# A hybrid decoder step: prompt attention heads whose transposes and products use four other PSUM banks, with ScalarE's exponentials moved ahead of its evictions

## The chip, the cores and the metric

The kernel runs on one core of one Trainium2 chip. The metric is the device time of one execution in microseconds (us). Five engines work side by side, each through its own list of instructions: TensorE (PE, with weight loads shown apart as PEld), VectorE (DVE), ScalarE (ACT), GpSimd (POOL) and SyncE (SP, which here only issues DMAs). They meet only at semaphores.

## The reference

One layer of a decoder trunk is applied to a prompt of 512 tokens and to a sample group of 8 sequences with 8 new tokens each, with the same weights. The part that matters here is the attention of the prompt. Every query keeps its 128 best keys (chosen by the indexer), and the softmax runs over these:

```python
logits = jnp.einsum('bthd,btkhd->bthk', q, k_sel).astype(jnp.float32) * ATT_SCALE
bias = rel_bias[rel_bucket(q_pos[None, :, None] - idx)]
logits = logits + jnp.swapaxes(bias, -1, -2).astype(jnp.float32)
logits = jnp.where(valid[:, :, None, :], logits, -jnp.inf)
p = jax.nn.softmax(logits, axis=-1).astype(v_sel.dtype)
out = jnp.einsum('bthk,btkhd->bthd', p, v_sel)
```

There are 8 heads of 128 columns, all in float32. Around it stand one wide input projection, the same attention of the sample group over 2,048 cached positions (paged keys and values, 64 MB each), a spatial gating branch, output projections and a convolutional feed-forward network.

## The kernel before

The program is written out engine by engine, in one block for each; nothing is scheduled automatically. The stages in the order of TensorE are: input transposes, indexer, the q, k and v projections, the eight prompt heads, the sample attention (two groups G, each with a loop over 17 pages of keys and four loops over pages of values), and the rest.

PSUM has eight banks of 128 x 512 float32. Banks 0 to 3 form two pairs; column tiles and row tiles of the projections fill them in turn (`pbank`, `ptile`). Banks 4 to 7 are single banks (`bank`), which are handed out strictly in the order of a list made at the top of the function: `single.add` gives each fill the next of the four banks. A fill waits until the previous use of its bank is drained (`claim`), and signals `single_filled` when done. The names of fills in this stage are `pl` (logits of head h, row block r), `pt` (the probabilities transposed) and `pv` (the product with the values).

The eight heads ("heads stage") are pipelined over h = 0 to 8. A head has four blocks of 128 query rows; block r sees 128 x (r + 1) keys (the causal half). For each h:

- TensorE (loop at L1214): logits of head h+1 (four matmuls, L1204), the product of head h-1 with the values (four matmuls, L1222), then ten 128 x 128 transposes of head h's probabilities (L1230).
- VectorE (L1861): reciprocal of the sums (L1862), four normalisations of the probabilities (L1865), then `prompt_max` for head h+1: for each row block, logits plus a bias mask with a running maximum (L1852), and one negation of the four maxima (L1856), which signals `max_ready`.
- ScalarE (L1560): eviction of the head's output (L1565, "oa"), four evictions of the transposed probabilities into the buffer `PT` (L1572), then the four exponentials of head h+1 (L1541), which signal `exp_done`.
- GpSimd (L899): the bias masks `MB` for the next head, four row blocks in six instructions (L905 to L909), each when VectorE has read the same block of the head before.

The logits buffers `L`, the maxima `MX`, `NM`, the sums `SU` and reciprocals `RC` exist twice (h % 2); `PT` and `MB` exist once. Behind the last head, TensorE does 32 steps of a "side" projection (`side_parts('start')`, columns `ga`), GpSimd clears `QB` (L933), ScalarE fills it (L1582), and the key loop begins with VectorE's transposes of key pages (L1910).

Apart from the heads, `sample_mask` (L1824 to L1843, 15 VectorE instructions, of 128 x 1032 in the larger ones) turns the sample group's best lists into a mask. It stands on VectorE between `prompt_max(0)` and the first normalisation.

## Time and profile before

| what | value |
|---|---|
| time of three runs | 1479.3, 1481.48 and 1484.05 us, median 1481.48 us |
| the profiled execution's own time | 1478.58 us |
| its span, first to last instruction | 1476.9 us |
| TensorE busy | 93% of the span |
| VectorE, ScalarE, GpSimd busy | 53%, 28%, 23% |
| heads stage | about 320 to 393 us of the span |
| mean granted TensorE clock | 0.969 |

The profile is of one execution. Busy shares are means over stages with different limits. The granted clock is a share of 2.4 GHz: 1.00 is 2.4 GHz and 0.50 is 1.2 GHz. "Idle before" is the time the engine stood idle directly before an instruction, with the instruction that released it. In the trace, a float32 matmul is two records, so a group of four matmuls is shown as x8.

### The profile page before, as it was taken

Reading aid. Unit: us, or ns where it says so; the run is one execution under the profiler, and the core shown is the slowest. Engines: PE = TensorE matmul, PEld = TensorE weight load, DVE = VectorE, ACT = ScalarE, POOL = GpSimd, SP = SyncE. Lnnn points to the kernel's source line nnn. Section 1 sums busy time; section 2 is a strip of 40 time slices with the busy share of each in tenths; the row PEclk is TensorE's granted clock in tenths of the full one; section 3 lists DMA queues with packets and bytes.
Section 4 is the critical chain, followed back from the end, with each engine's and each line's share of the span. In section 5 each row is a group of like instructions: output and inputs, shape, how many; then the busy total and the mean of one; then the engine's idle time right before and its main releaser. Section 6 shows DMA issues by size and latency. Waiting matters only on the chain.

```text
span 1476.9 us, 33784 instructions
## 1 busy us (share of the span) xinstructions
PE 1369.3 (93%) x14554; PEld 1228.4 (83%) x14554; DVE 788.7 (53%) x1117; ACT 417.2 (28%) x596; POOL 337.0 (23%) x427
## 2 busy tenths in 40 slices
PE   6989998987888999889999999999999999999997
PEld 4966798974677876578876698999999999999997
DVE  5278779444188820088820037444666676762221
ACT  4243322234521131011131141223333333332221
POOL 3613323424332100032100001322222222210000
PEclk8899999999999999999999999999999999999998
DMA  6415223230399899999899884142432223332332
GB/s 182 138 48 163 60 68 133 68 122 1 127 346 374 312 354 403 402 364 343 315 332 391 349 303 159 48 142 86 150 84 76 76 81 86 86 123 82 84 86 81
DMA packets 170624, 266.81 MB, mean 181 GB/s; under 512 B 19866, under 2 KB 136011, under 8 KB 161259
## 3 DMA queue, kind: packets, MB, share of 16 engines
q1 hardware_dynamic: 149275, 174.13, 35.1%
q0 software_dynamic: 14320, 78.22, 13.9%
q10 hardware_dynamic: 6880, 12.29, 2.4%
q8 instruction: 115, 1.88, 0.5%
q14 instruction: 34, 0.28, 0.1%
HBM read 240.30 MB, written 24.18 MB: 179 GB/s over the span
## 4 chain that ended last, share of the span: by engine, by line
PE 76%; DVE 10%; ACT 4%; DMA 4%; issue 3%; POOL 1%; SPq 1%; ACTq 0%; DVEq 0%; POOLq 0%
PE PS L1024 15%; PE PS L1026 14%; PE PS L1025 14%; PE PS L1257 5%; PE PS L1289 4%; PE PS L1366 3%; PE PS L1368 3%; PE PS L1367 3%; PE PS L1068 3%; DMA R<-in_cache_v 3%; DVE SR L1820 3%; DVE STG L1819 3%; PE PS L1069 2%; PE PS L1070 2%; PE PS L1222 1%
## 5 line engine op out<-in xcount | busy, mean ns | idle before, releaser
L1024 PE MATMUL PS<-xn_hi,WH 128*128 128x288 f32 (+1 forms) x1424 | 431.9, 303 | 6.2 <-DVE xn_lo L1702 3.8
L1026 PE MATMUL PS<-xn_hi,WL 128*128 128x288 f32 (+1 forms) x1424 | 421.7, 296 | 1.2 <-issue 1.2
L1025 PE MATMUL PS<-xn_lo,WH 128*128 128x288 f32 (+1 forms) x1424 | 421.7, 296 | 0.4 <-issue 0.3
L1024 PEld LDWEIGHTS PS<-xn_hi,WH 128*128 128x128 f32 (+1 forms) x1424 | 268.2, 188 | 24.4 <-issue 11.6
L1025 PEld LDWEIGHTS PS<-xn_lo,WH 128*128 128x128 f32 (+1 forms) x1424 | 268.6, 189 | 1.3 <-issue 1.3
L1026 PEld LDWEIGHTS PS<-xn_hi,WL 128*128 128x128 f32 (+1 forms) x1424 | 268.5, 189 | 1.4 <-issue 1.4
L604 DVE TENSOR_TENSOR WL<-W,WH 128x2048 fp32r<-128x2048 f32 (+2 forms) x73 | 154.8, 2120 | 181.2 <-ACT WH L1420 181.1
L1420 ACT ACTIVATE WH<-W 128x2048 fp32r<-128x2048 f32 (+2 forms) x81 | 144.9, 1789 | 105.1 <-PE PS L1368 74.8
L1460 ACT ACTIVATE STG<-PS 128x576 f32<-128x576 f32 (+2 forms) x44 | 23.4, 531 | 342.7 <-PE PS L1026 194.3
L657 POOL DMA_INDIRECT R<-in_cache_k,KROW x64 | 64.4, 1006 | 235.8 <-PE PS L1289 99.6
L1910 DVE STREAM_TRANSPOSE R<-R 128x2048 f32<-128x2048 f32 x42 | 96.0, 2295 | 20.1 <-PE PS L1257 16.2
L1068 PE MATMUL PS<-WH,xn_hi 128*128 128x256 f32 (+1 forms) x320 | 103.5, 323 | 3.2 <-ACT R L1559 3.2
L1366 PE MATMUL PS<-G_hilo,WH 128*128 128x288 f32 x352 | 104.2, 296 | 0.0
L1368 PE MATMUL PS<-G_hilo,WL 128*128 128x288 f32 x352 | 103.7, 295 | 0.0
L1367 PE MATMUL PS<-G_hilo,WH 128*128 128x288 f32 x352 | 103.7, 295 | 0.0
L1003 POOL COPY STH<-CV 128x2 f32<-128x2 f32 x44 | 51.5, 1170 | 199.4 <-DVE CV L2047 199.4
L1289 PE MATMUL PS<-R,R 128*32 128x128 f32 x2176 | 88.5, 281 | 8.3 <-DMA R<-in_cache_v 7.8
L1069 PE MATMUL PS<-WL,xn_hi 128*128 128x256 f32 (+1 forms) x320 | 91.4, 286 | 0.0
L1070 PE MATMUL PS<-WH,xn_lo 128*128 128x256 f32 (+1 forms) x320 | 91.3, 285 | 0.0
L1658 ACT ACTIVATE CV<-CV,VT 128x592 f32<-128x592 f32 x44 | 39.0, 887 | 173.1 <-DVE CV L2047 173.1
L1068 PEld LDWEIGHTS PS<-WH,xn_hi 128*128 128x128 f32 (+1 forms) x320 | 58.8, 184 | 27.3 <-issue 27.2
L1951 DVE TENSOR_SCALAR R<-PS,ST 128x128 f32<-128x128 f32 x16 | 4.9, 347 | 135.0 <-PE PS L1289 135.0
(295 smaller groups left out, 2420.0 us busy)
## 6 DMA issues: line engine op xcount, KB each, us to landing
R<-in_cache_v SPq DMA_DIRECT2D x128, 512.0 KB, 7.7
W<-in_w_in SPq DMA_DIRECT2D x30, 1024.0 KB
W<-in_w_up SPq DMA_DIRECT2D x44, 512.0 KB
W<-in_w_down SPq DMA_DIRECT2D x16, 704.0 KB
x_scratch<-xT SPq DMA_DIRECT2D x2, 2304.0 KB, 9.5
W<-in_w_branch_a SPq DMA_DIRECT2D x4, 1024.0 KB
W<-in_w_branch_b SPq DMA_DIRECT2D x4, 1024.0 KB
W<-in_w_out SPq DMA_DIRECT2D x4, 1024.0 KB
```

Of the source, the lines that this page charges most:

```text
L604: e.tensor_tensor(WL[n % NW][:, 0:c], W[n % NW][:, 0:c], WH[n % NH][:, 0:c].bitcast(F32), ALU.subtract).then_inc(low_count[name][0], 1)
L1024: pe.matmul(out, hi[:, k, cols], x.hi_block(n)[:, tokens], start=first, stop=False)
L1025: pe.matmul(out, hi[:, k, cols], x.lo_block(n)[:, tokens], start=False, stop=False)
L1026: return pe.matmul(out, lo[:, k, cols], x.hi_block(n)[:, tokens], start=False, stop=last)
L1068: pe.matmul(out, xn1.hi_block(k)[:, t], hi[:, k, :], start=(k == 0), stop=False)
L1069: pe.matmul(out, xn1.hi_block(k)[:, t], lo[:, k, :], start=False, stop=False)
L1070: end = pe.matmul(out, xn1.lo_block(k)[:, t], hi[:, k, :], start=False, stop=(k == KT - 1))
L1289: last = pe.matmul(bank('o', G, b)[32 * j:32 * j + 32, HD * u:HD * u + HD], PTs[:, u, kp, 32 * j:32 * j + 32], page[:, HD * h:HD * h + HD] ...
L1366: pe.matmul(out, hi[:, k, :], gated(n, 0)[:, t], start=(n == 0), stop=False)
L1367: pe.matmul(out, hi[:, k, :], gated(n, 1)[:, t], start=False, stop=False)
L1368: last = pe.matmul(out, lo[:, k, :], gated(n, 0)[:, t], start=False, stop=(n == FB - 1))
L1420: act.activation(WH[n % NH][:, 0:c], W[n % NW][:, 0:c], ACT.Copy).then_inc(S_("high_ready"), 1)
```

## The change

The `pt` and `pv` fills leave the four single banks. The transposes go to `TURNED` and the products to `HEAD_OUT`, which are fixed places in banks 0 to 3, those of the column tiles. Banks 4 to 7 now hold nothing but logits. The waits become counters of their own: `turned` (transposes of a row block written; block 0 and 1 share bank 0 and are signalled together), `turned_out` (evicted), `head_made` and `head_out`. Before the stage TensorE also waits for both last row tiles of v to be drained, and behind it the first side tile in banks 2 and 3 waits for the last `head_out`. ScalarE does head h+1's exponentials first, then the output of head h-1, then the transposed probabilities of head h. The negation of the maxima is four instructions of one column each in place of one of four, and every exponential waits for its own row block. On VectorE `sample_mask` goes ahead of `prompt_max(0)`.

```diff
@@ the list of fills @@
-        if h:
-            single.add('pv', h - 1)
-        if h < H:
-            for r in range(4):
-                single.add('pt', h, r)
@@ places @@
+        TURNED = [PS[:, 0, 0:128], PS[:, 0, 128:384], PS[:, 1, 0:384], PS[:, 2, :]]
+        HEAD_OUT = PS[:, 3, :]
@@ TensorE @@
             drained(pe, 'v', 3, 4)
+            drained(pe, 'v', 3, 3)
...
                 if h:
-                    drained(pe, 'pt', h - 1, 3)
-                    claim(pe, 'pv', h - 1)
+                    pe.wait_ge(S_("turned_out"), 4 * h)
+                    if h > 1:
+                        pe.wait_ge(S_("head_out"), h - 1)
                     for s in range(4):
-                        last = pe.matmul(bank('pv', h - 1)[:, P * s:TP], V[:, s, HD * (h - 1):HD * h],
+                        last = pe.matmul(HEAD_OUT[:, P * s:TP], V[:, s, HD * (h - 1):HD * h],
                                          PT[:, s, P * s:TP], start=(s == 0), stop=(s == 3), skip_group_check=True)
-                    done(last, 'pv', h - 1)
+                    last.then_inc(S_("head_made"), 1)
                 if h < H:
                     for r in range(4):
                         pe.wait_ge(S_("probs_ready"), 4 * h + r + 1)
-                        claim(pe, 'pt', h, r)
                         for s in range(r + 1):
-                            last = pe.transpose(bank('pt', h, r)[:, P * s:P * s + P],
+                            last = pe.transpose(TURNED[r][:, P * s:P * s + P],
                                                 L[h % 2][:, SP_OFF[r] + P * s:SP_OFF[r] + P * s + P], ident)
-                        done(last, 'pt', h, r)
+                        if r:
+                            last.then_inc(S_("turned"), 1)
@@ TensorE, side_parts @@
+                    if tile == side_first[1] and first == 0:
+                        pe.wait_ge(S_("head_out"), H)
@@ ScalarE @@
             def prompt_exp(h):
-                act.wait_ge(S_("max_ready"), h + 1)
                 for r in range(4):
                     n, o = P * (r + 1), SP_OFF[r]
+                    act.wait_ge(S_("max_ready"), 4 * h + r + 1)
...
             for h in range(H + 1):
+                if h + 1 < H:
+                    prompt_exp(h + 1)
                 if h:
-                    filled(act, 'pv', h - 1)
+                    act.wait_ge(S_("head_made"), h)
                     if h == 1:
                         act.wait_ge(S_("x_out"), 16)
-                    act.activation(oaT[:, h - 1, 0:TP], bank('pv', h - 1), ACT.Copy).then_inc(drains('pv', h - 1), 1)
+                    act.activation(oaT[:, h - 1, 0:TP], HEAD_OUT, ACT.Copy).then_inc(S_("head_out"), 1)
...
                     for r in range(4):
-                        filled(act, 'pt', h, r)
-                        act.activation(PT[:, 0:r + 1, P * r:P * r + P], blocks(bank('pt', h, r), 4)[:, 0:r + 1, :],
-                                       ACT.Copy).then_inc(drains('pt', h, r), 1)
-                    if h + 1 < H:
-                        prompt_exp(h + 1)
+                        act.wait_ge(S_("turned"), 3 * h + max(r, 1))
+                        act.activation(PT[:, 0:r + 1, P * r:P * r + P], blocks(TURNED[r], r + 1),
+                                       ACT.Copy).then_inc(S_("turned_out"), 1)
@@ VectorE @@
+            def negated(h, r):
+                drained(dve, 'pl', h, r)
+                dve.tensor_scalar(NM[h % 2][:, r:r + 1], MX[h % 2][:, r:r + 1], -1.0, None, ALU.mult)\
+                    .then_inc(S_("max_ready"), 1)
...
-                drained(dve, 'pl', h, 3)
-                dve.tensor_scalar(NM[h % 2], MX[h % 2], -1.0, None, ALU.mult).then_inc(S_("max_ready"), 1)
-
+                    if r:
+                        negated(h, r - 1)
+                negated(h, 3)
+
+            sample_mask()
             prompt_max(0)
-            sample_mask()
```

Three more waits elsewhere (`key_freed`, GpSimd ahead of clearing `QB`, VectorE ahead of its second key transpose) name `head_made` and `head_out` in place of `pv`; they wait for the same events.

On TensorE, in the second round of the heads (logits of head 2, product of head 0, transposes of head 1), the program before reads as follows. `L1204` are logits, `L1222` products and `L1230` transposes; `R_66` holds the logits and `PT`, and `single_drained0` to `3` are the four single banks.

```order
L1204 MATMUL PS<-R_63,R_64 128x128 [waits single_drained1]
L1204 MATMUL PS<-R_63,R_64 128x256 [waits single_drained2]
L1204 MATMUL PS<-R_63,R_64 128x384 [waits single_drained3]
L1204 MATMUL PS<-R_63,R_64 128x512 [waits single_drained0]
L1222 MATMUL PS<-R_66,R_63 128x512 [waits single_drained1,single_drained0]
L1222 MATMUL PS<-R_66,R_63 128x384
L1222 MATMUL PS<-R_66,R_63 128x256
L1222 MATMUL PS<-R_66,R_63 128x128
L1230 MATMUL PS<-CST,R_66 128x128 [waits single_drained2,probs_ready]
L1230 MATMUL PS<-CST,R_66 128x128 [waits single_drained3,probs_ready]
L1230 MATMUL PS<-CST,R_66 128x128
```

In the changed program the same instructions stand in the same order, as `L1206`, `L1226` and `L1233`.

```order
L1206 MATMUL PS<-R_63,R_64 128x128 [waits single_drained1]
L1206 MATMUL PS<-R_63,R_64 128x256 [waits single_drained2]
L1206 MATMUL PS<-R_63,R_64 128x384 [waits single_drained3]
L1206 MATMUL PS<-R_63,R_64 128x512 [waits single_drained0]
L1226 MATMUL PS<-R_66,R_63 128x512 [waits turned_out]
L1226 MATMUL PS<-R_66,R_63 128x384
L1226 MATMUL PS<-R_66,R_63 128x256
L1226 MATMUL PS<-R_66,R_63 128x128
L1233 MATMUL PS<-CST,R_66 128x128 [waits probs_ready] x2
L1233 MATMUL PS<-CST,R_66 128x128
L1233 MATMUL PS<-CST,R_66 128x128 [waits probs_ready]
```

What moved is the waits alone: the product no longer waits for a single bank (which VectorE's maxima of head 2 free) but for the evicted transposes, and the transposes wait for nothing but the probabilities.

On ScalarE, in the first two rounds (h = 0 and 1), the program before has the evictions of the transposed probabilities (`L1572`) ahead of the exponentials (`L1541`) and the output (`L1565`).

```order
L1572 ACTIVATE R_66<-PS 128x128 [waits single_filled,k_stored1,k_stored0]
L1572 ACTIVATE R_66<-PS 128x2x128 [waits single_filled]
L1572 ACTIVATE R_66<-PS 128x3x128 [waits single_filled]
L1572 ACTIVATE R_66<-PS 128x4x128 [waits single_filled]
L1541 ACTIVATE R_66,ST<-R_66,ST 128x128 [waits max_ready]
L1541 ACTIVATE R_66,ST<-R_66,ST 128x256
L1541 ACTIVATE R_66,ST<-R_66,ST 128x384
L1541 ACTIVATE R_66,ST<-R_66,ST 128x512
L1565 ACTIVATE oa<-PS 128x512 [waits x_out,single_filled]
L1572 ACTIVATE R_66<-PS 128x128 [waits single_filled]
L1572 ACTIVATE R_66<-PS 128x2x128 [waits single_filled]
L1572 ACTIVATE R_66<-PS 128x3x128 [waits single_filled]
```

In the changed program (`L1545` exponentials, `L1578` transposed probabilities, `L1571` output) the same place reads:

```order
L1545 ACTIVATE R_66,ST<-R_66,ST 128x128 [waits max_ready]
L1545 ACTIVATE R_66,ST<-R_66,ST 128x256 [waits max_ready]
L1545 ACTIVATE R_66,ST<-R_66,ST 128x384 [waits max_ready]
L1545 ACTIVATE R_66,ST<-R_66,ST 128x512 [waits max_ready]
L1578 ACTIVATE R_66<-PS 128x128 [waits turned,k_stored1,k_stored0]
L1578 ACTIVATE R_66<-PS 128x2x128 [waits turned]
L1578 ACTIVATE R_66<-PS 128x3x128 [waits turned]
L1578 ACTIVATE R_66<-PS 128x4x128 [waits turned]
L1545 ACTIVATE R_66,ST<-R_66,ST 128x128 [waits max_ready]
L1545 ACTIVATE R_66,ST<-R_66,ST 128x256 [waits max_ready]
L1545 ACTIVATE R_66,ST<-R_66,ST 128x384 [waits max_ready]
L1545 ACTIVATE R_66,ST<-R_66,ST 128x512 [waits max_ready]
```

The exponentials of head 1 and head 2 each moved one block up, ahead of the evictions, and each now carries a wait of its own.

On VectorE, at head 0's maxima, the changed program has these rows (`ISA` of 128 x 128 to 128 x 512 are the maxima, `ISA ST` the read of the maximum, `L1852` the negations, and `L1872` the reciprocal):

```order
L1861 ISA R_66,ST<-PS,R_66 128x128 [waits single_filled,bias_mask_ready]
L1861 ISA ST 128x1
L1861 ISA R_66,ST<-PS,R_66 128x256 [waits single_filled,bias_mask_ready]
L1861 ISA ST 128x1
L1852 TENSOR_SCALAR ST<-ST 128x1 [waits single_drained1]
L1861 ISA R_66,ST<-PS,R_66 128x384 [waits single_filled,bias_mask_ready]
L1861 ISA ST 128x1
L1852 TENSOR_SCALAR ST<-ST 128x1 [waits single_drained2]
L1861 ISA R_66,ST<-PS,R_66 128x512 [waits single_filled,bias_mask_ready]
L1861 ISA ST 128x1
L1852 TENSOR_SCALAR ST<-ST 128x1 [waits single_drained3]
L1852 TENSOR_SCALAR ST<-ST 128x1 [waits single_drained0]
```

Before, the four maxima stood together with one negation of 128x4 behind them, and `sample_mask` between it and the reciprocal.

## Rows read from the trace of the kernel before

**Rows 1.** Windows, core 0: length, busy us of each engine, PE clock, DMA share, GB/s.
```profile
320.50:332.90 12.40, 7.91 (x27) 4.80 (x27) 4.56 (x17) 3.96 (x13) 9.43 (x15) 0.86 0.79 275
332.90:393.00 60.10, 45.19 (x174) 29.93 (x175) 21.75 (x83) 27.80 (x83) 25.17 (x34) 0.89 0.10 35
352.00:354.00 2.00, 2.00 (x8) 1.53 (x6) 0.00 (x0) 0.18 (x1) 1.82 (x3) 0.50 0.00 0
411.00:450.00 39.00, 36.47 (x849) 32.59 (x850) 35.45 (x27) 5.14 (x4) 13.26 (x13) 0.94 1.00 367
```

**Rows 2.** Timeline of PE: start us, us, what, count [idle before].
```profile
320.57 2.43 PE L1204 MATMUL PS<-R,R 128*128 128x128 f32 x8 [0.47 <-ACT R L1559]
...
327.99 3.37 PE L1204 MATMUL PS<-R,R 128*128 128x128 f32 x8
332.89 2.39 PE L1222 MATMUL PS<-R,R 128*128 128x512 f32 x8 [1.53 <-DVE ST L1852]
335.12 1.57 PE L1230 MATMUL PS<-CST,R 128*128 128x128 f32 x10
336.53 2.32 PE L1204 MATMUL PS<-R,R 128*128 128x128 f32 x8
341.38 2.39 PE L1222 MATMUL PS<-R,R 128*128 128x512 f32 x8 [2.53 <-DVE ST L1852]
...
349.87 3.91 PE L1222 MATMUL PS<-R,R 128*128 128x512 f32 x8 [2.53 <-DVE ST L1852]
...
379.93 3.25 PE L1222 MATMUL PS<-R,R 128*128 128x512 f32 x8 [2.87 <-DVE ST L1852]
...
385.77 2.42 PE L1222 MATMUL PS<-R,R 128*128 128x512 f32 x8 [0.69 <-ACT R L1572]
388.49 1.64 PE L1230 MATMUL PS<-CST,R 128*128 128x128 f32 x10 [0.29 <-DVE R L1865]
390.82 2.42 PE L1222 MATMUL PS<-R,R 128*128 128x512 f32 x8 [0.69 <-ACT R L1572]
```

**Rows 3.** Waits from 318 to 412 us: total, times, longest.
```profile
PE PS L1222 <- DVE ST L1852: 14.5, 6, 2.9
```

**Rows 4.** Timeline of DVE in the heads stage.
```profile
327.00 0.74 DVE L1856 TENSOR_SCALAR ST<-ST 128x4 f32<-128x4 f32 x1
...
339.75 1.27 DVE L1865 TENSOR_SCALAR R<-R,ST 128x128 f32<-128x128 f32 x4
...
341.97 0.69 DVE L1852 CUSTOM_DVE_ANT_0 R<-PS,R 128x512 f32<-128x512 f32 x1
...
342.70 0.17 DVE L1856 TENSOR_SCALAR ST<-ST 128x4 f32<-128x4 f32 x1
...
361.27 2.29 DVE L604 TENSOR_TENSOR WL<-W,WH 128x2048 fp32r<-128x2048 f32 x1
```

**Rows 5.** Timeline of ACT around one head.
```profile
335.32 0.60 ACT L1565 ACTIVATE oa<-PS 128x512 f32<-128x512 f32 x1 [4.30 <-PE PS L1222]
335.82 1.51 ACT L1572 ACTIVATE R<-PS 128x128 f32<-128x128 f32 x4
...
338.71 0.71 ACT L1541 ACTIVATE R<-R,ST 128x512 f32<-128x512 f32 x1
339.32 0.19 ACT L1541 ACTIVATION_READ_ACCUMULATOR R<-R,ST 128x1 f32 x1
```

**Rows 6.** Timeline of POOL: one head's bias masks, and one that met a split.
```profile
341.31 0.45 POOL L907 TENSOR_TENSOR R<-R,RB 128x128 f32<-128x128 f32 x1 [4.48 <-DVE ST L1852]
...
344.60 0.72 POOL L909 TENSOR_TENSOR R<-R,RB 128x256 f32<-128x256 f32 x1
...
361.50 2.65 POOL L909 TENSOR_TENSOR R<-R,RB 128x256 f32<-128x256 f32 x1
```

**Rows 7.** The chain that ended last, behind the last head.
```profile
393.29 0.61 ACT oa L1565
...
408.58 2.31 DVE RB L1910
```

More of the change, by code:

```diff
@@ L571, in key_freed @@
             elif n == 2:
-                filled(e, 'pv', H - 1)
+                e.wait_ge(S_("head_made"), H)
                 e.wait_ge(S_("v_stored"), 32)
@@ L930, in _ @@
             load_keys(pool, 0, 1)
-            filled(pool, 'pv', H - 1)
-            drained(pool, 'pv', H - 1)
+            pool.wait_ge(S_("head_made"), H)
+            pool.wait_ge(S_("head_out"), H)
             pool.memset(QB, 0.0).then_inc(S_("queries_cleared"), 1)
@@ L1072, in row_tile @@
                     done(end, kind, c, r)
+            side_first = {pair.slots[tile][0]: tile for tile in side[1::-1]}
             def column_tile(kind, c, first=0, last=2 * KT):
@@ L1899, in transposed @@
                             if G == 0:
-                                filled(dve, 'pv', H - 1)
+                                dve.wait_ge(S_("head_made"), H)
                             else:
```

## The prediction

> **What bounds the kernel now.** I read the table of windows first, to see which stage has slack; then the timelines of the four engines through that stage, side by side; then the waits, for what ends TensorE's idle time; last the chain behind the stage, to see whether time saved there reaches the end.
>
> In the heads stage TensorE is busy for 45.2 of 60.1 us at a granted clock of 0.89, with ScalarE, VectorE and GpSimd each under half busy and the DMA share at 0.10 [rows 1]. So it is bound neither by an engine nor by transfers, but by a loop of waits. The loop is visible in one head of 8.49 us, product start to product start (332.89 to 341.38) [rows 2]: the product (2.39), the transposes (1.57), and the evictions on ScalarE; only then ScalarE's exponentials, then VectorE's reciprocal and normalisations, then its maxima of the next head. The next product stands idle for 2.53 us until these maxima begin [rows 2], although it needs nothing of them: it waits for the bank that holds that head's logits. Such waits sum to 14.5 us over six products [rows 3].
>
> A second loss follows. With 8.49 us a head TensorE has 2.32 + 2.39 + 1.57 = 6.3 us of work, and from the third product on the granted clock falls during it: 0.50 (1.2 GHz) at 352 us [rows 1], and the product takes 3.91 and later 3.25 in place of 2.39 us [rows 2]. Four products are that slow, from 349.87 to 379.93.
>
> Behind the stage, ScalarE's last output (end at 393.90) releases, through clearing and filling `QB`, the key pages' transposes at 408.58 [rows 7], and from 411 us on the DMA share is 1.00 [rows 1]. The transfers of that stage start only after the heads: the share is 0.10 while they run. So a stage that ends earlier lets the transfers start earlier by as much.
>
> **The change, part by part.** I work on the profiled execution: its span is 1476.9, its own time 1478.58, and the median of the runs is 1481.48, so the execution shown is 2.9 us below the median. I subtract the gain from the median.
>
> (a) First product. `prompt_max(1)` is paced by GpSimd's bias masks, which start behind v's stores; the change leaves them. VectorE's negation of head 1 starts at 327.00 [rows 4]. In the changed order the exponentials of blocks 0 and 1 are gone by then and blocks 2 and 3 follow: to about 327.2 with the negations, then some 0.6 for block 2 and 0.71 + 0.19 less overlap for block 3 [rows 5], so 328.6. Then come the four evictions of head 0, 1.51 [rows 5], and the first product at 330.2. Before it is at 332.89: 2.7 us won, though the evictions now stand behind the exponentials.
>
> (b) The steady heads. If the maxima no longer hold the product, TensorE's own work is the period. Start to start, the product occupies it for 335.12 - 332.89 = 2.23 and the transposes for 336.53 - 335.12 = 1.41 [rows 2]; the logits I take at 2.32 less the same tail of 0.16, 2.16. Sum 5.80. Do the others keep up? GpSimd's six instructions of a head run from 341.31 to 345.32, 4.0 us [rows 6]. ScalarE has 0.5 of output, 1.5 of evictions and, from their end at 337.33 to 339.51, 2.2 of exponentials [rows 5], 4.2. VectorE has 0.24 for the reciprocal (339.51 to 339.75), 1.27 for the normalisations, 1.7 for four maxima (341.02 to 342.70, the largest 0.69) and four negations of 0.17 in place of one [rows 4, 5], 3.9. The loop through both: from the end of a head's logits 0.8 (last maximum), 0.2 (negation), 0.9 (last exponential), 0.2 and 1.27, with some 0.3 of semaphores, is 3.7 us, and the next logits are complete after 5.8. The evictions: the exponentials end 1.9 + semaphores behind the logits, about when the 2.23 us product does, so the output and the 1.5 us of evictions end before the following logits do. Five periods from the first product make the sixth start at 330.2 + 29.0 = 359.2; before it is at 379.93.
>
> (c) The tail has no logits to cover the evictions. Seventh product: 2.23 + 1.57 + 0.69 (the gap that is seen now) = 4.5, at 363.7. Eighth: 2.42, then output 0.5 and evictions 1.5 in ScalarE's order and 0.15 of semaphores, 4.6, at 368.3. End 370.7, against 390.82 + 2.42 = 393.24 [rows 2]. That is 22.5 us.
>
> (d) The new wait ahead of the first side tile: its bank pair is the one with `HEAD_OUT`, so TensorE stands for the last output, 0.61 [rows 7] and a semaphore, 0.7 us. I cost it at nothing: TensorE waits for the key transposes at 408.58 anyway. If that cover were gone it would cost 0.7.
>
> (e) `sample_mask` ahead of head 0's maxima: VectorE has nothing else to do there, and the first transposes follow head 1's logits at 320.57 [rows 2]. Nothing; were it to delay GpSimd's split of a v chunk, the bound is one held instruction, 2 us, as in the 2.65 for 0.72 of [rows 6].
>
> (f) Clock. The first round still has idle time in front of it, and the logits at 327.99 already took 3.37 for 2.32 [rows 2]. One product at the lower clock costs 3.91 - 2.39 = 1.5. I take the 1.5; the bounds are none and four such products, 6.
>
> (g) VectorE and GpSimd in each other's way. GpSimd's bias masks now run beside negations and normalisations. The negation at 327.00 took 0.74, the one at 342.70 took 0.17 [rows 4], and a GpSimd addition beside VectorE's 2.29 us split took 2.65 for 0.72 [rows 4, 6]. The lower bound is nothing. The upper is that each of the four negations loses 0.57 and the normalisations wait for some 1.5: 3.8 us a head, of which the slack of (b), 5.8 - 3.7 less the maxima that must follow, about 1.3, hides a part; 2.5 x 5 = 12 us. I take 1.5, near the low end, since only the two early blocks' negations meet additions.
>
> Sum: 22.5 - 1.5 - 1.5 = 19.5, so 1481.5 - 19.5 = 1462.
>
> Page of the Trainium skill, SBUF — State Buffer, "Who interferes with whom": VectorE in a two-port mode and GpSimd lock each other out for whole instructions, whoever issues first. By this the normalisations beside bias masks would also be held, and (g) would be at its upper end. The 2.65 us addition agrees; the 0.17 us negation beside a running GpSimd instruction doesn't.
>
> **The rivals.**
> - *The pair of VectorE and GpSimd sets the pace* ((g) at its upper end): 22.5 - 1.5 - 12 = 9 us won, 1472. For it the 0.74 and 2.65; against it the 0.17 at 342.70 with GpSimd at work [rows 4, 6], and that normalisations never met a bias mask so far. Chance 0.13.
> - *The stage shrinks and the end does not move.* The key and value stage runs at a DMA share of 1.00 [rows 1]; if its end were set by something that doesn't start with the heads' end, the gain would be given back as waiting for pages. Time 1481. Against it the share of 0.10 before. Chance 0.05.
> - *ScalarE's queue closes into one serial loop, slower.* The exponentials, which wait for maxima, now stand ahead of the output and the evictions. If the next head's logits came late, everything would follow in turn: logits 2.16, maximum and negation 1.2, exponential 0.9, output 0.6, evictions 1.5, product 2.4, transposes 1.6 = 10.4 us a head, where now (393.24 - 320.57) / 8 = 9.1 pass. Eight heads: 10 us slower, 1492. It decides from a period of 9.1. Against it: TensorE issues the logits of head h+2 before the product of head h, so they don't wait for that chain. Chance 0.05.
>
> **How the numbers follow.** The forecast (14 to 24 us won, 1457 to 1468) has 0.77. The low end is (g) at nothing and (f) at nothing with some 3 us of scatter between runs, 1481.5 - 22.5 - 3 = 1456; the high end takes in most of the first rival, 1473. A measurement tells 0.3%, 4.4 us, from no change. Faster 0.90 (forecast and first rival), same 0.05, slower 0.05.
>
> **What would show it.** Product starts 5.8 to 6.5 us apart and no idle time ahead of products but the first and the last two; the first at about 330; clock 1.00 from 335 to the stage's end; the last product's end at 371 to 375; key transposes at 386 to 389. (a) is wrong if the first product is later than 331.5; (b) if products still wait for ScalarE; (g) if negations take over 0.3 us on average or bias masks over 5 us a head. The prediction is wrong as a whole if the stage ends 20 us earlier but the last page of values doesn't.

## The result, and the profile after

The changed kernel takes **1463.53 us** (median of 4 runs, 1459.62 to 1467.02), the kernel before 1482.76 us (median of 4, 1479.3 to 1484.76). The ratio is 0.9868, with a 95% interval of 0.9837 to 0.9899: 15 to 24 us are won. The forecast was 1462. The profiled execution took 1462.85 us, its span is 1461.2 us and its mean clock 0.972.

The windows of the changed kernel, with the columns of [rows 1], show the heads stage first.

```profile
320.50:330.00 9.50, 6.38 (x27) 3.69 (x28) 3.77 (x16) 3.83 (x13) 9.16 (x14) 1.00 0.92 308
330.00:375.00 45.00, 41.44 (x198) 29.21 (x199) 26.99 (x105) 29.49 (x89) 28.67 (x37) 0.96 0.16 58
393.00:450.00 57.00, 49.05 (x1171) 43.93 (x1174) 46.95 (x38) 6.44 (x6) 16.93 (x16) 0.97 1.01 373
```

TensorE is busy for 92% of the stage where it was busy for 75% [rows 1], and the clock is 0.96, not 0.89. The page stage behind it runs at the full DMA share as before, but starts earlier.

The timeline of TensorE shows the new loop.

```profile
320.58 2.42 PE L1206 MATMUL PS<-R,R 128*128 128x128 f32 x8 [0.47 <-ACT R L1563]
...
327.02 1.12 PE L1206 MATMUL PS<-R,R 128*128 128x512 f32 x2 [0.82 <-DVE ST L1861]
329.83 4.11 PE L1226 MATMUL PS<-R,R 128*128 128x512 f32 x8 [1.68 <-ACT R L1578]
333.79 1.26 PE L1233 MATMUL PS<-CST,R 128*128 128x128 f32 x10
334.88 2.32 PE L1206 MATMUL PS<-R,R 128*128 128x128 f32 x8
337.04 2.32 PE L1226 MATMUL PS<-R,R 128*128 128x512 f32 x8
...
342.45 2.32 PE L1226 MATMUL PS<-R,R 128*128 128x512 f32 x8
...
353.26 2.32 PE L1226 MATMUL PS<-R,R 128*128 128x512 f32 x8
...
358.93 2.42 PE L1226 MATMUL PS<-R,R 128*128 128x512 f32 x8
...
364.31 2.42 PE L1226 MATMUL PS<-R,R 128*128 128x512 f32 x8 [1.86 <-ACT R L1578]
...
368.74 2.42 PE L1226 MATMUL PS<-R,R 128*128 128x512 f32 x8 [0.91 <-ACT R L1578]
371.85 0.40 PE L1022 MATMUL PS<-xn_hi,WH 128*128 128x288 f32 x1 [0.69 <-ACT oa L1571]
```

From 337.04 to 353.26 the products stand 5.41 us apart (three periods: 342.45 - 337.04 = 5.41, and 353.26 - 342.45 = 10.81 for two), where the first ones stood 8.49 apart [rows 2], and no wait is written behind them. The sixth, at 358.93, comes after 5.67. Three of the eight still wait, the first and the last two, and for ScalarE's evictions, not for VectorE's maxima. The first product takes 4.11 us: the mean granted clock from 329.80 to 334 us is 0.59, so most of it ran at the lower level (0.50), behind 1.68 us of idle time and the two shorter gaps before it.

The view of waits, from 318 to 392 us, sums this up.

```profile
ACT R L1545 <- DVE ST L1852: 13.3, 9, 3.4
DVE R L1861 <- POOL R L905: 11.7, 1, 11.7
DVE ST L1872 <- ACT R L1545: 8.1, 6, 1.4
PE PS L1226 <- ACT R L1578: 4.5, 3, 1.9
```

The 14.5 us of [rows 3] are gone, and 4.5 us stand in their place. ScalarE and VectorE still wait for each other, but TensorE no longer stands with them. The 11.7 us are VectorE in front of the first mask.

On ScalarE a steady head's evictions stand at 339.95, and the last output, which [rows 7] showed at 393.29, stands at 371.20.

```profile
339.95 1.40 ACT L1578 ACTIVATE R<-PS 128x128 f32<-128x128 f32 x4
...
371.20 0.60 ACT L1571 ACTIVATE oa<-PS 128x512 f32<-128x512 f32 x1 [2.51 <-PE PS L1226]
```

The evictions end at 341.35 and TensorE's product begins at 342.45: there is 1.1 us of room in each head. In the chain that ended last the key transposes begin at 386.44, where they began at 408.58 [rows 7].

```profile
386.44 2.31 DVE RB L1920
```

Both marks lie 22.1 us earlier than before (393.29 - 371.20 = 22.09, 408.58 - 386.44 = 22.14): the heads' gain passes whole to the page stage.

VectorE's timeline tells what the sharing with GpSimd costs: a negation, the normalisations of a steady head, a weight split with the normalisations of head 5 behind it, and those of head 7.

```profile
331.92 0.14 DVE L1852 TENSOR_SCALAR ST<-ST 128x1 f32<-128x1 f32 x1
...
334.43 1.85 DVE L1875 TENSOR_SCALAR R<-R,ST 128x128 f32<-128x128 f32 x4
...
348.97 2.28 DVE L602 TENSOR_TENSOR WL<-W,WH 128x2048 fp32r<-128x2048 f32 x1
351.17 0.17 DVE L1872 RECIPROCAL ST<-ST 128x4 f32<-128x4 f32 x1
351.37 2.44 DVE L1875 TENSOR_SCALAR R<-R,ST 128x128 f32<-128x128 f32 x4
...
362.72 1.27 DVE L1875 TENSOR_SCALAR R<-R,ST 128x128 f32<-128x128 f32 x4
```

GpSimd's bias masks at the same places:

```profile
331.61 0.73 POOL L907 TENSOR_TENSOR R<-R,RB 128x256 f32<-128x256 f32 x1
...
334.48 0.73 POOL L907 TENSOR_TENSOR R<-R,RB 128x256 f32<-128x256 f32 x1
...
349.00 2.84 POOL L907 TENSOR_TENSOR R<-R,RB 128x256 f32<-128x256 f32 x1
351.82 0.92 POOL L903 TENSOR_SCALAR R<-R,RB 128x256 f32<-128x256 f32 x1
```

The negation at 331.92 runs beside an addition of GpSimd and takes 0.14 us. The normalisations at 334.43, beside GpSimd too, take 1.85 us; those of head 7, when no mask is left to make, 1.27 us as in [rows 4]. At 348.97 the split holds GpSimd (0.73 becomes 2.84). GpSimd is then late, and head 5's normalisations, beside the rest of its mask, take 2.44 us.

### The profile page after: what moved, and what is told of

Its sections match the earlier page's. It is cut to its first block, busy times and chain, and to the rows that moved or that the text cites. A ratio compares the mean times of both kernels' runs of the same rounds, so it can differ in the third digit from the quotient of the medians.

```text
span 1461.2 us, 33775 instructions
## 1 busy us (share of the span) xinstructions
PE 1360.6 (93%) x14554; PEld 1225.1 (84%) x14554; DVE 796.6 (55%) x1141; ACT 416.3 (28%) x596; POOL 335.3 (23%) x427
## 4 chain that ended last, share of the span: by engine, by line
PE 75%; DVE 11%; DMA 4%; issue 4%; ACT 4%; POOL 1%; SPq 1%; ACTq 0%; DVEq 0%; POOLq 0%
PE PS L1022 15%; PE PS L1024 14%; PE PS L1023 14%; PE PS L1261 5%; PE PS L1293 5%; PE PS L1066 3%; PE PS L1372 3%; PE PS L1370 3%; PE PS L1371 3%; DVE SR L1824 3%; DVE STG L1823 3%; PE PS L1067 2%; PE PS L1068 2%; DMA R<-in_cache_v 2%; PE PS L1172 1%
```

## The experiments

There are eight experiments, two of them the kernels of before and after once more. The first four experiments share runs of the kernel before (median 1483.65 us of 11 runs), the last four others (1483.14 us of 11). Two questions stood: which part of the change wins the time, and what each of the small terms is worth. My theory was that the freed bank alone does it (theory 1 in the expectations); the first rival was that ScalarE's new order is needed or is the true cause.

**banks_only.** The banks part alone. ScalarE's order, the single negation and `sample_mask` stand as before.

```diff
 # against the changed kernel, ScalarE:
-                if h + 1 < H:
-                    prompt_exp(h + 1)
                 if h:
                     act.wait_ge(S_("head_made"), h)
...
+                    if h + 1 < H:
+                        prompt_exp(h + 1)
 # VectorE:
-                    if r:
-                        negated(h, r - 1)
-                negated(h, 3)
+                drained(dve, 'pl', h, 3)
+                dve.tensor_scalar(NM[h % 2], MX[h % 2], -1.0, None, ALU.mult).then_inc(S_("max_ready"), 1)
...
+            prompt_max(0)
             sample_mask()
-            prompt_max(0)
```

The wait inside `prompt_exp` goes back to one for all four row blocks with it.

> The banks part of the change alone: transposes and products in banks 0 to 3, with ScalarE's order, the one negation of 128x4 and the place of the sample mask as in the kernel before. Theory 1 (the release of the bank is nearly all of the gain): products start some 5.4 to 5.8 us apart, the last product ends at 370 to 373 us of the span (393.2 before, 371.2 in the changed kernel), and the time is that of the changed kernel within 3 us, about 1463. The first product even starts some 2 us earlier than in the changed kernel, near 328, since head 0's evictions don't stand behind head 1's exponentials. Theory 2 (the exponentials ahead of the evictions are needed for the overlap): the loop through evictions, exponentials and normalisations stays closed, products stay 7 us or more apart, the last product ends after 380 us, and at most half of the gain is left, about 1473.

Measured: 1461.65 us (1459.04 to 1466.86, 4 runs), ratio 0.9861 (0.9821 to 0.9901). TensorE's timeline:

```profile
327.44 2.32 PE L1226 MATMUL PS<-R,R 128*128 128x512 f32 x8
330.11 1.65 PE L1233 MATMUL PS<-CST,R 128*128 128x128 f32 x10 [0.35 <-DVE R L1874]
...
333.75 2.32 PE L1226 MATMUL PS<-R,R 128*128 128x512 f32 x8
335.91 1.54 PE L1233 MATMUL PS<-CST,R 128*128 128x128 f32 x10
...
339.44 2.32 PE L1226 MATMUL PS<-R,R 128*128 128x512 f32 x8
...
368.07 2.42 PE L1226 MATMUL PS<-R,R 128*128 128x512 f32 x8 [0.69 <-ACT R L1576]
```

The waits for the maxima are gone with the old order too, and the period is 5.69 us. The last product begins 48.0 us behind the first logits (320.03), in the changed kernel 48.2. So the banks alone give the whole gain. The way there differs: the first product follows on its logits without a gap, 7.4 us behind the first logits and not 9.25, and runs at the full clock, and the longer periods give this back.

**order_only.** The rest of the change alone: exponentials first, a negation for each row block, `sample_mask` early; the banks and their list as before.

```diff
 # against the kernel before, ScalarE (and the negations and sample_mask as in the change):
+                if h + 1 < H:
+                    prompt_exp(h + 1)
                 if h:
                     filled(act, 'pv', h - 1)
...
-                    if h + 1 < H:
-                        prompt_exp(h + 1)
```

> The other part alone: exponentials ahead of the evictions, a negation for each row block and the sample mask ahead of head 0's maxima, with the single banks handed out as in the kernel before. Theory 1 (the bank's wait is the cause): products still wait for the maxima of the next head, but these come earlier, since the exponentials start without the evictions ahead of them; products 6.4 to 6.9 us apart, last product ends at 375 to 379 us, time 1466 to 1470, so most of the gain could be had in this way too and the two parts don't add. Theory 2 (the two parts are each worth a part of the gain and add): last product ends near 383 us, half of the gain, about 1473.

Measured: 1466.06 us (1461.68 to 1468.57, 4 runs), ratio 0.9885 (0.9847 to 0.9923).

```profile
330.24 4.04 PE L1204 MATMUL PS<-R,R 128*128 128x128 f32 x8 [0.95 <-ACT R L1574]
334.11 2.32 PE L1222 MATMUL PS<-R,R 128*128 128x512 f32 x8
...
339.89 2.32 PE L1222 MATMUL PS<-R,R 128*128 128x512 f32 x8
...
372.51 2.42 PE L1222 MATMUL PS<-R,R 128*128 128x512 f32 x8 [0.69 <-ACT R L1574]
```

The period is 339.89 - 334.11 = 5.78 us, and the products before the seventh don't wait. With the exponentials ahead of the evictions VectorE gets the sums earlier, and is through with the maximum that frees the product's bank before the product comes up: this maximum begins at 338.26, 1.6 us ahead of the product at 339.89, where in the kernel before it began at 340.94 and the product, held by it, at 341.38. So the rival was half right: the order alone opens the loop too. Its start is worse. The first product stands 12.0 us behind the first logits (322.12) against 7.4 in banks_only, and 1.7 of this are the logits at the lower clock (4.04 us for 2.32). The two parts don't add: 17.6 us alone (1483.65 - 1466.06), 22.0 alone (1483.65 - 1461.65), and 17.8 for both in the run that follows. The differences between these three are within their intervals.

**after_again.** The changed kernel once more, unchanged, beside these.

> The changed kernel once more, for a second trace and a closer ratio. Ratio to the kernel before 0.985 to 0.989. The heads stage repeats: last product ends at 371.2 within 0.5 us, 22 us earlier than before. Theory A (6 us of those 22 are lost behind the stage in every execution, by the wait for the reload of the gate tensor and what follows): the lead over the trace of before is 21 us at the last value page, about 17 to 18 us behind the first branch projection, and 16 us at the end. Theory B (the loss is chance, where TensorE's clock falls in one execution and not in the other): the lead at the end differs from 15.7 us by more than 2 us in this trace.

Measured: 1465.86 us (1461.93 to 1471.31, 6 runs), ratio 0.9881 (0.9848 to 0.9915). The last output stands at 373.06, but the stage began later too, its first logits at 322.45. Counted from there it is 50.6 us, the same as in the first trace (371.20 - 320.58). So I count all stages from their first logits from here on. The lead over the first trace of before is 11.2 us at the end (1476.9 - 1465.7) and not 15.7, so by the mark set in advance theory B holds: what is lost or won behind the heads differs from one execution to the next.

**head_out_bank0.** Step (d) by itself: the product's bank moves to the other pair, so that the new wait stands elsewhere.

```diff
-        TURNED = [PS[:, 0, 0:128], PS[:, 0, 128:384], PS[:, 1, 0:384], PS[:, 2, :]]
-        HEAD_OUT = PS[:, 3, :]
+        TURNED = [PS[:, 1, 0:128], PS[:, 1, 128:384], PS[:, 2, 0:384], PS[:, 3, :]]
+        HEAD_OUT = PS[:, 0, :]
...
-                    if tile == side_first[1] and first == 0:
+                    if tile == side_first[0] and first == 0:
```

> The changed kernel with the output's bank and the transposes' banks exchanged: products in bank 0, transposes in banks 1 to 3. The first side tile, which is in banks 2 and 3, then needn't wait for the last output, and only the second one would. If the wait costs nothing (the prediction's step d): the first side matmul starts 0.7 us earlier behind the last product, the key transposes stay where they are within 0.1 us (386.4), and the time is the same. If it costs: key transposes and time 0.7 us earlier.

Measured: 1467.47 us (1466.71 to 1467.73, 4 runs), ratio 0.9889 (0.9852 to 0.9927). From the last output to the key transposes it is 15.2 us (372.24 to 387.48), as in the changed kernel (371.20 to 386.44). The first side matmul follows here without a wait, so the 0.69 us that TensorE waits there in the changed kernel cost nothing at the end. The stage itself is 0.8 us shorter (49.9 from first logits). Head 5's normalisations were held less here, 1.80 us and not 2.44, and the sixth product shows no delay. VectorE doesn't touch the banks that were exchanged, so I don't put this down to the edit, but no run separates it from chance. Head 5's normalisations:

```profile
353.18 1.80 DVE L1875 TENSOR_SCALAR R<-R,ST 128x128 f32<-128x128 f32 x4
```

**before_again.** The kernel before once more, for its trace: in the first pair of traces the lead of 22.1 us shrank to 15.7 by the end of the span (1476.9 - 1461.2), and I wanted to know where. Either the change lost it behind the heads, or the first trace of before was a lucky one.

> The kernel before once more, for its trace. Behind the heads, the five traces of kernels with a shorter heads stage take 67.6 to 68.3 us from the last output transposes of the sample attention to the first spatial gating matmul; the trace of before takes 64.8 (848.8 to 913.6). Theory A (the shortened stage costs this stage 3 us): again 64.5 to 65.5 here. Theory B (the one trace of before was lucky in this stage, and nothing is lost behind the heads): 67 to 68.5 here, and the span is near 1480. The heads stage repeats: products 8.5 us apart at first and 9.8 to 10.2 from the third on, last output 72 to 73 us behind the first logits.

Measured: 1478.96 us in one run, span 1477.3. Its products repeat [rows 2], with three slow ones (3.80, 3.46 and 3.87 us) for four:

```profile
338.15 2.39 PE L1222 MATMUL PS<-R,R 128*128 128x512 f32 x8 [2.52 <-DVE ST L1852]
...
346.64 3.80 PE L1222 MATMUL PS<-R,R 128*128 128x512 f32 x8 [2.52 <-DVE ST L1852]
...
386.20 2.42 PE L1222 MATMUL PS<-R,R 128*128 128x512 f32 x8 [0.69 <-ACT R L1572]
```

The stage is 71.3 us from first logits to last output, 72.7 in the first trace. The stretch from the sample attention's last output to the first spatial gating matmul, 64.8 us in the first trace of before and 68.3 in that of after, took 67.8 here. In the eight traces with a shorter heads stage it took 67.6 to 68.4. So that stretch was the larger half of the shrinking (3.5 of 6.4), and with 67.8 in an unchanged kernel nothing points to the change; the first trace of before was the lucky one there (theory B).

**no_bias.** What GpSimd costs, step (g). Left out: the bias masks of heads 2 to 7; these heads are computed with head 1's.

```diff
-            for h in range(1, H):
+            for h in range(1, 2):
                 bias_mask(h)
...
-                    dve.wait_ge(S_("bias_mask_ready"), 4 * h + r + 1)
+                    dve.wait_ge(S_("bias_mask_ready"), 4 * min(h, 1) + r + 1)
```

> The changed kernel without GpSimd's bias masks of heads 2 to 7, which leaves this part of the computation out: these heads are computed with head 1's mask. It takes GpSimd away from beside VectorE. If GpSimd holds VectorE's normalisations (step g of the prediction): the four normalisations of a head take 1.27 us in place of 1.85, the first one 1.27 in place of 2.19, and the period of the products stays 5.41 us, since it is TensorE's own work; the last product ends 1 to 2.6 us earlier through the first round, head 5 and the tail. If GpSimd isn't the cause, the normalisations stay at 1.85 us.

Measured: 1457.89 us in one run.

```profile
330.51 2.42 PE L1226 MATMUL PS<-R,R 128*128 128x512 f32 x8 [1.68 <-ACT R L1578]
...
336.02 2.32 PE L1226 MATMUL PS<-R,R 128*128 128x512 f32 x8
...
341.43 2.32 PE L1226 MATMUL PS<-R,R 128*128 128x512 f32 x8
...
362.01 2.42 PE L1226 MATMUL PS<-R,R 128*128 128x512 f32 x8 [0.95 <-ACT R L1578]
```

Every group of normalisations takes 1.27 to 1.30 us, so GpSimd is what holds them. The period is 5.41 us all the same: the slack hides it in the steady heads. What it costs shows at the end, where the seventh product waits 0.95 us and not 1.86. The stage is 47.7 us, 3.0 shorter (50.62 - 47.65). Of these, 4.11 - 2.42 = 1.7 are the first product's clock, which didn't fall here, and 1.3 are left for GpSimd.

**bias1_early.** The other end of that: the idle time before the first product comes from head 1's bias mask, which GpSimd begins behind v's stores. Here it makes this mask before it.

```diff
+            bias_mask(1)
             drained(pool, 'v', 3, 4)
...
-            for h in range(1, H):
+            for h in range(2, H):
                 bias_mask(h)
```

> The changed kernel with head 1's bias mask made ahead of the stores of v on GpSimd, which stands idle there, instead of behind them. Theory: the first round is paced by this mask (maxima of head 1 at 322.7, 323.4, 324.7 and 326.3 us wait for it), so the first product starts near 326.5 in place of 329.8 and everything behind it 3 to 4 us earlier: last product ends at 367 to 368 us, counted from first logits at 320.6. The time is 3 to 4 us lower than the changed kernel's in the span up to the key transposes; in the total perhaps the same within its scatter. Rival: the first round is paced by TensorE's or ScalarE's own order, and the start of the first product moves by less than 1 us.

Measured: 1465.38 us (1459.81 to 1467.25, 4 runs), ratio 0.9882 (0.9844 to 0.992).

```profile
321.90 2.42 PE L1207 MATMUL PS<-R,R 128*128 128x128 f32 x8 [0.47 <-ACT R L1564]
...
328.03 2.42 PE L1227 MATMUL PS<-R,R 128*128 128x512 f32 x8 [0.46 <-ACT R L1579]
```

The first product stands 6.1 us behind the first logits (9.25 before), and runs at the full clock. The stage takes 46.2 us, 4.4 less than in the changed kernel. The median shows nothing of it: each ratio's interval is some 0.007 wide, 10 us.

**banks_rows_bias1.** What the runs point to: the kernel of bias1_early (the banks, a negation for each row block, `sample_mask` and head 1's mask early), but with ScalarE in its old order, since banks_only started better and waited 0.69 us before its last two products, not 1.86 and 0.91.

> The version that the runs so far point to: banks 0 to 3 for transposes and products, a negation for each row block, the sample mask early and head 1's bias mask early, but ScalarE's order as before, evictions ahead of the next head's exponentials. Worked out from measured durations: first product 5 us behind the first logits (326), last product ends at 366.8, that is 4.4 us ahead of the changed kernel and 0.5 to 1 us ahead of bias1_early; total 1458 to 1460 where the changed kernel has 1463. If ScalarE's new order were worth something in company with the early mask, this one would end later than bias1_early.

Measured: **1460.3 us** (1456.13 to 1466.05, 6 runs), ratio 0.9853 (0.9823 to 0.9884).

```profile
326.23 2.32 PE L1207 MATMUL PS<-R,R 128*128 128x128 f32 x8
328.39 2.32 PE L1227 MATMUL PS<-R,R 128*128 128x512 f32 x8
...
333.80 2.32 PE L1227 MATMUL PS<-R,R 128*128 128x512 f32 x8
...
350.03 2.32 PE L1227 MATMUL PS<-R,R 128*128 128x512 f32 x8
...
356.00 2.32 PE L1227 MATMUL PS<-R,R 128*128 128x512 f32 x8
```

No product waits before the seventh, the first follows directly on its logits, and the period is 5.41 us from the first to the fifth. The sixth comes after 5.97, since the transposes before it took 1.76 us for 1.25. It has the shortest stage, and the lowest median of all kernels that do the whole work. Its interval overlaps that of the changed kernel, so I don't call it faster.

All stages side by side, in us. The second column runs from the first logits to the last output, the third from there to the end of the span.

| kernel | heads stage | last output to the end | median |
|---|---|---|---|
| before, two traces | 72.7, 71.3 | 1083.6, 1088.6 | 1482.76, 1483.65 and 1483.14 |
| changed, two traces | 50.6, 50.6 | 1090.0, 1092.6 | 1463.53, 1465.86 |
| banks_only | 50.5 | 1086.9 | 1461.65 |
| order_only | 52.9 | 1085.1 | 1466.06 |
| head_out_bank0 | 49.9 | 1092.9 | 1467.47 |
| no_bias | 47.7 | 1087.1 | one run, 1457.89 |
| bias1_early | 46.2 | 1093.7 | 1465.38 |
| banks_rows_bias1 | 45.6 | 1091.3 | 1460.3 |

The third column, a stretch in which only the places and names of a few waits were edited, spreads over 10 us. That is more than the largest difference among the changed versions' stages (52.9 - 45.6 = 7.3), and it doesn't follow the second column. Most of the spread lies in the sample attention: from its first key transposes to its last output transposes, the ten traces take 439.4 to 445.8 us.

## Why the prediction was right, step by step

**The bound.** A loop of waits through the shared bank, not an engine: right. banks_only changes where the products and the transposes go and nothing else, and all waits for the maxima go with it. Which of the two users had to leave the rotation, no run tells: they were moved together.

**(a) First product**: 330.2 forecast, 329.83 measured. Right, with ScalarE's four evictions behind the exponentials (328.39 to 329.78).

**(b) The steady heads**: 5.80 forecast, 5.41 measured, below the 5.8 to 6.5 that the prediction named as its sign. The mechanism was right. The term was mis-sized by the transposes, which I took at the 1.41 us of [rows 2]; they occupy 334.88 - 333.79 = 1.09. The 0.3 us between them are a wait that the change takes away as well. In the old list the fourth block's bank is the one that the product before it has just filled, and ScalarE must first evict the output from it.

```profile
343.81 0.60 ACT L1565 ACTIVATE oa<-PS 128x512 f32<-128x512 f32 x1 [4.30 <-PE PS L1222]
```

In the kernel before, this eviction ends at 344.41; six of the transposes behind the product at 341.38 start from 343.61 on, and the last four at about 344.6. In order_only, with the same list, the last four stand apart in every group that has logits behind it. In two of these groups the profile names this eviction; in the others it names VectorE, whose normalisations of that head had long ended.

```profile
354.59 0.63 PE L1230 MATMUL PS<-CST,R 128*128 128x128 f32 x4 [0.17 <-ACT oa L1567]
```

In banks_only the group takes 1.37 us (335.91 to 337.28) for another reason: its normalisations come at the same time (335.46 to 336.73), and the period is 5.69. The loop of VectorE and ScalarE is not longer than the period, as forecast.

**(c) The tail**: the seventh product was put 4.5 us behind the sixth and came after 5.38; the eighth at 4.6 came after 4.43. The sixth is at 358.93 for a forecast of 359.2, the last at 368.74 for 368.3. In the new order the evictions of head 6 come behind head 7's exponentials, and these behind head 6's normalisations and head 7's maxima on VectorE, so a late normalisation reaches this product. That is the step to which (g) belongs. In the old order, in banks_only and banks_rows_bias1, the gap before the seventh is the 0.69 that I took, but the transposes before it wait for normalisations instead: from the sixth product to the eighth it is 10.65 and 10.05 us there, and 9.81 in the changed kernel, for 9.1 forecast. So the old order wins at the start of the stage, not in its tail.

**(d) and (e)**: right. The wait is there, 0.69 us, and head_out_bank0 shows it to be worth nothing; `sample_mask` stands on VectorE, which waits 11.7 us for the first mask anyway, and head 1's maxima start at 322.73 as they did before (322.72).

**(f) Clock**: 1.5 forecast, 4.11 - 2.32 = 1.8 measured, on one product, as forecast. The clock was 1.00 from 334 us to the stage's end. That there is one such product and not none is not sure: in banks_only, no_bias and both kernels with head 1's mask early there is none.

**(g) VectorE and GpSimd**: 1.5 forecast; no_bias gives 1.3. The size was right, the instructions were not, so the size was luck. I had negations held, and no single-column negation was (0.14 or 0.15 us each, all 32). The four-column one of the kernel before took 0.74 us at the same place in banks_only and 0.94 in before_again, for 0.17 elsewhere; cut into four it isn't held there. The normalisations were held, by 0.92 us in head 1 (2.19 for 1.27), by 0.54 to 0.59 in each steady head (1.81 to 1.86), which is hidden, and by 1.17 in head 5, which is not. It takes both parts of the change to put the steady heads' normalisations beside the masks: in heads 2 to 4 they take 1.27 or 1.28 us in banks_only and banks_rows_bias1, and 1.27 to 1.31 in order_only. The rival with its 12 us had the normalisations right, but at 1.5 us a head, nearly three times what they lost, and less slack than there is: the steady period shows nothing of the 0.54 to 0.59 us.

The Trainium skill's page SBUF — State Buffer, "Who interferes with whom", says that `tensor_scalar` can enter a two-port mode and then locks GpSimd out or is locked out, and that an instruction of VectorE with one SBUF input outside these modes isn't. By this rule the normalisations are held and the maxima, which read PSUM and one SBUF tile, aren't. The traces agree on both: 1.85 and 1.27 us for the one, and for the largest maximum 0.67 to 0.69 us beside masks in the changed kernel and 0.68 or 0.69 in no_bias, where there are none. The one-column negation is the same operation as the normalisation and was never held. The 2.65 us addition, which the prediction set beside this rule, belongs elsewhere: a split is a `tensor_tensor`, which by the same section has no two-port mode, but contends with GpSimd's reads by its two SBUF inputs.

**The sum.** Adding the stage up from the forecast's undisturbed end of 370.7: -0.4 for (a), -1.95 for (b) (5 periods of 0.39), +1.8 for (f), and +1.0 for (g) and the tail (0.26 before the sixth product, 0.88 before the seventh, -0.17 before the eighth) give 371.15; measured is 371.16 (368.74 + 2.42). So the stage gained 22.1 us where I had 19.5 with (f) and (g) in it, and (b) with (a) paid for most of both. Some 3 of the 22 us are the clock, by an estimate from the rows: in the first trace of before the three periods from the third product on are 10.01, 9.85 and 10.20 us for 8.49, 4.6 us more, and the changed kernel loses 1.8.

The medians show 19.2, and the forecast of 1462 against 1463.53 owes its closeness in part to luck: the stage won 2.6 us more than forecast, and 2.9 us of that gain are not in the medians. These 2.9 us stay open. Against the second trace of before, with 71.3 us, the stage gained only 20.7, which closes half of it. Behind the heads, the eight traces with an opened loop take 1090.0 us on average and the two of before 1086.1; with a scatter of 10 us, these runs don't tell whether some 3 us are given back there or nothing is. The bounds that the prediction works out at its end, 1456 and 1473, are not quite those it states (1457 and 1468); the measured time lies within both.

The rival in which the end doesn't move is out: 19 of 22 arrived, and the sample attention's last output transposes came 21.2 us earlier (848.8 and 827.6). One reading behind it was too coarse. The DMA share of 0.10 is a mean: from 380 to 393 us, in the stage's last 13 us, it was 0.44 before the change already, so the transfers don't wait for the end of the heads altogether.

**The other rivals.** The serial loop of ScalarE would have needed a period of 9.1 us; the logits were never late and the period was 5.41.

## What to carry to other kernels

When an engine waits for something that it doesn't need, look at what its destination bank is waiting for: an order of banks written for one pipeline ties unrelated steps together, and taking users out of it removed the waits here without any reordering. Reordering the other engines opened the same loop (the stage fell to 52.9 us, with the banks alone to 50.5). Two edits that open the same loop don't add, so each should be run alone; here one of them, with the simpler order on ScalarE, does it all. And compare a stage of 50 us in the traces, from its own first instruction: in the total, 4.4 us of it went under in 10 us of scatter behind it.

## What the runs showed of the hardware that I had not expected

The same gap before the first product cost different clocks. Behind 1.68 us of idle time it took 4.11, 4.12 and 4.12 us in after, after_again and head_out_bank0, and 2.42 us in no_bias, behind the same 1.68 us and at the same distance from the first logits (9.26 and 9.25 us). One run of no_bias doesn't tell whether this is chance or the missing masks.

A split of weights can reach TensorE 10 to 15 us later, through two engines. At 348.97 VectorE's split held a mask's addition for 2.84 us; the rest of that mask then met head 5's normalisations and held them for 1.17 us, when the split had already used up VectorE's slack. In head_out_bank0 the same split held a mask's addition for as long (2.85 us), but the masks held these normalisations for only 0.53 us, and the sixth product came 0.26 and the seventh another 0.49 us earlier (5.41 and 4.89 behind the one before, for 5.67 and 5.38).
